# One score matrix per half in the expert retrieval: query weights times keys, built in the kernel, for heads 4 to 7 behind the first tile's sums

## What is computed

```python
def chunk(xc):                                    # xc: normed tokens
    q = (xc @ w_query).reshape(PEER_CHUNK, PEER_HEADS, 2, PEER_HALF)      # 8 heads, 2 halves, 128
    s = jnp.einsum('thcd,hckd->thck', q, keys)                            # 128 keys per half
    top_s, top_i = lax.top_k(s, PEER_TOPK)                                # 16 of each half
    cand_s = top_s[:, :, 0, :, None] + top_s[:, :, 1, None, :]
    cand_i = top_i[:, :, 0, :, None] * N_KEYS + top_i[:, :, 1, None, :]
    best_s, best_j = lax.top_k(cand_s, PEER_TOPK)                         # 16 of the 256 pairs
    idx = jnp.take_along_axis(cand_i, best_j, axis=-1)
    gate = jax.nn.softmax(best_s, axis=-1)
    act = gelu(jnp.einsum('thkd,td->thk', u_table[idx], xc))
    return jnp.einsum('thk,thkd->td', gate * act, v_table[idx])
```

## Time and profile before

| | us |
|---|---|
| median of 3 runs | 3325.18 (3314.89 to 3326.9) |
| the profiled execution, timed | 3328.39 |
| its span in the trace | 3326.6 |
| PE busy, in the span | 2289.7 |
| DVE busy | 2177.2 |
| ACT busy | 936.3 |
| POOL busy | 1330.7 |
| 1088 gathers, 1143 MB, share of 16 DMA engines | 84.0% of the span |

### The profile page before, as it was taken

How to read it: one execution, slowest core, us unless ns; L and a number is a source line. 1 busy time by engine, 2 the same in 40 slices (tenths; PEclk the granted TensorE clock), 3 DMA queues, 4 the chain that set the end, 5 groups by cost and what they waited for, 6 DMA issues and landing times.

```text
span 3326.6 us, 31891 instructions
## 1 busy us (share of the span) xinstructions
PE 2289.7 (69%) x9269; PEld 938.1 (28%) x9269; DVE 2177.2 (65%) x5175; ACT 936.3 (28%) x3200; POOL 1330.7 (40%) x1272
## 2 busy tenths in 40 slices
PE   8997675766685668566855685568566855685576
PEld 4555451331151115111511151115111511151121
DVE  4544539788667756775677567756776676568654
ACT  2222114323332222222322232322232223222222
POOL 1241014434443444344434443444444444444442
PEclk9999787886896779687978797889688978797799
DMA  5223269999999999999999999999999999999998
GB/s 192 84 72 88 75 270 358 386 386 402 419 419 415 417 400 417 416 417 402 419 416 417 400 419 415 416 398 419 413 413 418 419 402 420 397 408 411 420 420 338
DMA packets 188351, 1216.94 MB, mean 366 GB/s; under 512 B 27272, under 2 KB 30712, under 8 KB 47456
## 3 DMA queue, kind: packets, MB, share of 16 engines
q0 software_dynamic: 157600, 1143.05, 84.0%
q1 hardware_dynamic: 30576, 71.86, 6.0%
HBM read 1199.15 MB, written 15.55 MB: 365 GB/s over the span
## 4 chain that ended last, share of the span: by engine, by line
DMA 33%; PE 22%; DVE 17%; issue 7%; ACT 5%; POOL 3%; another core or an unknown queue 0%; DVEq 0%; POOLq 0%; PEldq 0%; ACTq 0%; SPq 0%
DMA uv_ring<-in_uv_table,idx 33%; PE ACC L1998 14%; DVE uv_ring L1823 9%; PE TQ L1937 5%; POOL uv_ring L1465 3%; ACT dg L1598 2%; PE OP L1918 1%; ACT dot L1591 1%; PE TQ L1959 1%; ACT dot L1578 1%; DVE pos L1668 1%; DVE idx_f L1744 1%; DVE pos L1665 1%; DVE S L1743 1%; DVE best L1667 0%
## 5 line engine op out<-in xcount | busy, mean ns | idle before, releaser
L1998 PE MATMUL ACC<-uv_ring,dg 128*64 128x512 f32 x4352 | 1440.2, 772 | 932.5 <-ACT dg L1598 932.3
L1465 POOL DMA_INDIRECT uv_ring<-in_uv_table,idx x1088 | 1234.1, 1134 | 1611.2 <-PE ACC L1998 1375.1
L1823 DVE CUSTOM_DVE_ANT_0 uv_ring<-uv_ring,xn 128x1024 f32<-128x1024 f32 x1088 | 1326.5, 1226 | 738.2 <-DMA uv_ring<-in_uv_table,idx 675.5
L1998 PEld LDWEIGHTS ACC<-uv_ring,dg 128*64 128x64 f32 x4352 | 339.4, 164 | 1925.4 <-ACT dg L1598 1405.6
L1578 ACT ACTIVATE dot<-dot 128x2 f32<-128x2 f32 x544 | 110.5, 203 | 1853.6 <-DVE dot L1823 1838.8
L1598 ACT ACTIVATE dg<-stack,dot 128x64 f32<-128x64 f32 x1088 | 326.4, 340 | 17.8
L1591 ACT ACTIVATE dot<-gate,dot 128x1 f32<-128x1 f32 x1088 | 261.1, 287 | 18.9
L1937 PEld LDWEIGHTS TQ<-glu_and_queries,wq 128*128 128x128 f32 x2048 | 237.0, 194 | 63.9 <-issue 63.9
L1937 PE MATMUL TQ<-glu_and_queries,wq 128*128 128x128 f32 x2048 | 250.5, 281 | 0.0
L527 PE MATMUL PJ<-w_in,xT 128*128 128x512 f32 (+1 forms) x384 | 142.7, 528 | 3.2 <-DVE pj L407 3.2
L527 PEld LDWEIGHTS PJ<-w_in,xT 128*128 128x128 f32 x384 | 72.2, 191 | 68.1 <-issue 65.2
(11 more groups left out here) (336 smaller groups left out, 1640.2 us busy)
## 6 DMA issues: line engine op xcount, KB each, us to landing
uv_ring<-in_uv_table,idx POOLq DMA_INDIRECT x1088
glu_and_queries<-in_w_glu SPq DMA_DIRECT2D x9, 1024.0 KB
wq<-in_w_query SPq DMA_DIRECT2D x8, 1024.0 KB, 19.5
w_in<-in_w_in SPq DMA_DIRECT2D x8, 640.0 KB, 11.0
xt<-in_x SPq DMA_DIRECT2D x9, 512.0 KB, 4.7
xr<-scratch_x SPq DMA_DIRECT2D x9, 512.0 KB
xc<-in_x_columns SPq DMA_DIRECT2D x8, 512.0 KB, 3.8
xk<-in_x SPq DMA_DIRECT2D x8, 512.0 KB, 3.5
```

The source lines that it names most:

```text
L1465: pool.indirect_dma_start(out=ring[:, s_ % RING, :], out_offset=None, in_=a["uv_table"], in_offset=bass.IndirectOffsetOnAxis(ap=idx[:, s_: ...
L1823: V.tensor_tensor_reduce(row, row, xn[:, g, :], 1.0, 0.0, ALU.mult, ALU.add, dot[:, s_:s_ + 1]).then_inc(dots, 1)
L1998: ins = nc.tensor.matmul(ACC[GT * g:GT * (g + 1), b, :], dg[:, n % DG, :], ring[:, n % RING, D + 512 * b:D + 512 * b + 512], start=False, ...
```

## The change

Scores are linear in the tokens: s = (x W) K^T = x (W K^T). The kernel after makes W K^T once, a matrix of 1024 x 128 for each of the 16 head halves (`score_w`), and each tile's scores come from `xnT` and `score_w` without queries. In detail:

- Host layout: the query weights are handed over turned, so that the part of 128 of a half's queries lies on partitions; the bytes are the same. `keys` comes in four blocks for two heads each, two of which fit in SBUF at a time.
- `make_weights(n)` builds a quarter of a head's weights: four matmuls of 128 columns, of a block of turned query weights and the keys, into one PSUM bank. `take_weights(n)` copies the bank over the query weights that it came from. For n under 16 (heads 0 to 3) the banks are the two of `ACC`; for later ones it is bank 1 of `TQ`.
- Heads 0 and 1 are built within tile 0's own preparation: head 0 behind the gating matmuls at (0, 9), head 1 behind the bottom projection at (2, 3). Heads 2 and 3 follow behind the scores of heads 0 and 1 and behind both `spread_rows`. Heads 4 to 7 are built behind tile 0's sums: at pairs 4 to 7, 10 to 13, 16 to 19, 22 to 25, one quarter a pair, and their scores in the two pairs behind each.
- Tile 0's scores of a head are eight matmuls of 256 columns. Later tiles: at the steps where queries stood, two matmuls of 512 columns a step, 32 in all; the copies to `S` stand at (3, 12) and (5, 0).
- VectorE: head 3's piece A moves from ahead of the first product to slot 7, pieces A of heads 4 to 7 from slots 10, 18, 27, 36 to 25, 37, 49, 61; B to D follow. C and C2 use 8 rows of `S` instead of twice 4 of `quarter`.
- Tile 1's steps follow a table, `FIRST_STEPS`: none up to slot 8, 50 up to slot 60, step 72 at slot 80, step 83 at slot 88, and 45 in the 30 slots behind.
- `w_glu` has memory of its own and is loaded once. On SP the first keys and head 0's query weights go ahead of `w_bot`, `xr` and `g_ffn`; head 1's follow. New waits: TensorE ahead of each quarter waits for an earlier copy (`taken`), and ahead of tile 1's transposes for all copies; ScalarE waits for `made`; ahead of the copy of tile 1's first scores it waits for all of tile 0's indices.

The core of the diff:

```diff
-        wq = c.sb("wq", [P, EH, KD, 2 * QH])
-        keys = c.sb("keys", [QH, HC, KEYS])
+        score_w = c.sb("score_w", [P, HC, KD, KEYS])
+        wq_rows = score_w[:].rearrange("p c k n -> p c (k n)")
+        keys = c.sb("keys", [QH, 2, 4, KEYS])
         w_bot = c.sb("w_bot", [P, SW // P, D])
-        glu_and_queries = c.sb("glu_and_queries", [P, 2 * KD * P])
-        w_glu = glu_and_queries[:].rearrange("p (k n) -> p k n", n=SW)
-        xnT = glu_and_queries[:, 0:KD * P].rearrange("p (k n) -> p k n", n=P)
-        qT = glu_and_queries[:, KD * P:].rearrange("p (k n) -> p k n", n=P)
+        w_glu = c.sb("w_glu", [P, SW // P, SW])
+        xnT = c.sb("xnT", [P, KD, P])
...
-            lo, hi = 3 * KS + 3, NSLOT - 10
-            return s_ if s_ < lo else min(NSLOT, lo + (s_ - lo) * (NSLOT - lo) // (hi - lo))
+            for (s0, n0), (s1, n1) in zip(FIRST_STEPS, FIRST_STEPS[1:]):
+                if s0 <= s_ < s1:
+                    return n0 + (s_ - s0) * (n1 - n0) // (s1 - s0)
+            return NSLOT
...
+        FIRST_STEPS = ((0, 0), (8, 0), (60, 50), (69, 59), (71, 64), (80, 72), (84, 80), (88, 83), (NSLOT - 10, NSLOT))
+        BEFORE = 4
+        LATE_AT = {e: 4 + 6 * (e - BEFORE) for e in range(BEFORE, EH)}
+        TOP_AT = {3: 7} | {e: 2 * at + 17 for e, at in LATE_AT.items()}
+        BEST_AT = {1: 3, 2: 9, 3: 16} | {e: at + 3 for e, at in TOP_AT.items() if e >= BEFORE}
+        FIRST_HEADS = {at + n: (e, piece) for e, at in BEST_AT.items()
+                       for n, piece in ((0, "B"), (2, "C"), (3, "C2"), (5, "D"))}
+        FIRST_HEADS |= {at: (e, "A") for e, at in TOP_AT.items()}
...
+                def load_keys(n):
+                    if n >= 2:
+                        sp.wait_ge(made, QUARTERS * 2 * (n - 1))
+                        sp.nop(nofuse=True)
+                    sp.dma_start(keys[:, n % 2].rearrange("d c n -> d (c n)"), a["keys"][n]).then_inc(keys_in[n % 2], 16)
+                def load_queries(e):
+                    sp.dma_start(wq_rows[:, 2 * e:2 * e + 2], a["w_query"][e]).then_inc(wq_in[e], 16)
...
+                load_keys(0)
+                load_queries(0)
                 sp.dma_start(w_bot[:], a["w_out"][AW:D, :].rearrange("(k p) n -> p k n", p=P)).then_inc(bottom, 16)
                 load_xr(0)
                 sp.dma_start(g_ffn[:], a["g_ffn"].to_broadcast([P, D])).then_inc(bottom, 16)
...
+                load_queries(1)
+                load_keys(1)
+                sp.dma_start(place[:].rearrange("p n k -> p (n k)"), a["place"].to_broadcast([P, 2 * KS])).then_inc(tables_in, 16)
+                sp.dma_start(spread[:].rearrange("p g n -> p (g n)"), a["spread"]).then_inc(tables_in, 16)
+                for e in range(2, EH):
+                    load_queries(e)
...
+                def take_weights(n):
+                    c_, k0 = n // 2, n % 2 * (KD // 2)
+                    src = ACC[:, n % 2, :] if n < QUARTERS * BEFORE else TQ[:, 1, :]
+                    act.wait_ge(made, n + 1)
+                    A(score_w[:, c_, k0:k0 + KD // 2, :].rearrange("p k n -> p (k n)"), src, ACT.Copy).then_inc(taken, 1)
+                def late_heads(pair):
+                    for e, at in LATE_AT.items():
+                        if at < pair <= at + QUARTERS:
+                            take_weights(QUARTERS * e + pair - at - 1)
+                        elif pair == at + QUARTERS + 2:
+                            first_scores(e)
+                            if e == EH - 1:
+                                for n in ("S_a", "S_b", "ex_done"):
+                                    act.sem_inc(k[n].sem, 1)
...
+                        if (h, j) == (0, 14):
+                            for n in range(QUARTERS):
+                                take_weights(n)
+                for n in range(QUARTERS, 2 * QUARTERS):
+                    take_weights(n)
                 prepare(0, 3, 2)
...
+                first_scores(0)
+                first_scores(1)
+                for g in range(GROUPS):
+                    take_rows(0, g)
+                for e in range(2, BEFORE):
+                    for n in range(QUARTERS * e, QUARTERS * (e + 1)):
+                        take_weights(n)
                     first_scores(e)
...
+                    if e == 2:
+                        first_gates(0)
...
-                        n = KS // 4
-                        for k0 in range(0, KS // 2, n) if piece == "C" else range(KS // 2, KS, n):
-                            dch_(V.tensor_tensor(quarter[:], first_cid[:].to_broadcast([P, n, NCAND]),
-                                                 bcast(pos_f[:, e, k0:k0 + n], NCAND, 2), ALU.subtract))
-                            dch_(V.tensor_reduce(idx_f[:, e, k0:k0 + n], quarter[:], AX.X, ALU.min, apply_absolute_value=True))
+                        n, k0 = KS // 2, KS // 2 * (piece == "C2")
+                        dch_(V.tensor_tensor(first_match, first_cid[:].to_broadcast([P, n, NCAND]),
+                                             bcast(pos_f[:, e, k0:k0 + n], NCAND, 2), ALU.subtract))
+                        dch_(V.tensor_reduce(idx_f[:, e, k0:k0 + n], first_match, AX.X, ALU.min, apply_absolute_value=True))
...
-                for e in range(1, 4):
+                for e in range(1, 3):
...
+                        n, bank, part = "ab"[h == 4], i // 4, i % 4
                         if i == 0:
                             k["xnT_done"].of(pe, t)
...
+                            if n == "a":
+                                k["zb_done"].of(pe, t)
+                                k["S_b"].of(pe, t - 1)
+                            else:
+                                k["S_a"].of(pe, t)
+                        c_ = 8 * (h == 4) + 4 * bank
+                        for m in range(2 * part, 2 * part + 2):
+                            ins = nc.tensor.matmul(ZS[:, bank, :], xnT[:, m, :], score_w[:, c_:c_ + 4, m, :],
+                                                   start=(m == 0), stop=(m == KD - 1))
+                        if i == 7:
+                            k[f"s_{n}"].mark(ins)
...
+                def make_weights(n):
+                    e, c_, k0 = n // QUARTERS, n // 2, n % 2 * (KD // 2)
+                    if n < QUARTERS * BEFORE:
+                        dst, free = ACC[:, n % 2, :], n - 1
+                    else:
+                        dst, free = TQ[:, 1, :], n
+                    if n % QUARTERS == 0:
+                        pe.wait_ge(wq_in[e], 16)
+                        pe.wait_ge(keys_in[e // 2 % 2], 16 * (e // 4 + 1))
+                    if free > 0:
+                        pe.wait_ge(taken, free)
+                    for m in range(KD // 2):
+                        ins = nc.tensor.matmul(dst[:, m * KEYS:(m + 1) * KEYS],
+                                               wq_rows[:, c_, (k0 + m) * P:(k0 + m + 1) * P],
+                                               keys[:, e // 2 % 2, c_ % 4, :], start=True, stop=True)
+                    ins.then_inc(made, 1)
+                def first_scores(e, m0, m1):
+                    b = e % 2 if e < BEFORE else 1
+                    if m0 == 0:
+                        pe.wait_ge(taken, QUARTERS * (e + 1))
+                        if e >= 2:
+                            pe.wait_ge(first["S"], e - 1 if e < BEFORE else e)
+                    for m in range(m0, m1):
+                        ins = nc.tensor.matmul(ZS[:, b, 0:2 * KEYS], xnT[:, m, :], score_w[:, 2 * e:2 * e + 2, m, :],
+                                               start=(m == 0), stop=(m == KD - 1))
+                    if m1 == KD:
+                        ins.then_inc(first["s"], 1)
+                def late_heads(pair):
+                    for e, at in LATE_AT.items():
+                        n = pair - at
+                        if 0 <= n < QUARTERS:
+                            if (e, n) == (BEFORE, 0):
+                                k["xn_taken_b"].of(pe, 0)
+                            make_weights(QUARTERS * e + n)
+                        elif QUARTERS <= n < QUARTERS + 2:
+                            m0 = (n - QUARTERS) * (KD // 2)
+                            first_scores(e, m0, m0 + KD // 2)
...
+                        if (h, j) in ((0, 9), (2, 3)):
+                            e = int(h == 2)
+                            for n in range(QUARTERS * e, QUARTERS * (e + 1)):
+                                make_weights(n)
                 k["xnT_done"].of(pe, 0)
...
+                pe.wait_ge(tables_in, 16 * 2)
+                first_scores(0, 0, KD)
+                first_scores(1, 0, KD)
+                for g in range(GROUPS):
+                    spread_rows(0, g)
+                for e in range(2, BEFORE):
+                    for n in range(QUARTERS * e, QUARTERS * (e + 1)):
+                        make_weights(n)
+                    first_scores(e, 0, KD)
```

148 lines of the change are left out of this document (43 added, 105 removed).

## The result

The changed kernel takes 3292.49 us (median of 5 runs, 3290.23 to 3297.64), the kernel before, in the same rounds, 3323.84 us (5 runs, 3314.89 to 3326.9). The ratio is 0.992, with a 95% interval of 0.9903 to 0.9938: faster by 31 us (21 to 32 by the interval), where 50 had been forecast. 3292.5 lies inside the range of 3257 to 3296, near its upper end. The profiled execution of the changed kernel has a span of 3290.7 us, against 3326.6.

What follows compares the result with a forecast made beforehand. The prediction took the stream of gathers on the DMA engines as the bound: its start, dry spells and other bytes. Gains of 27.5 (start), 6.5 (tile 0) and 16 us (later tiles) sum to 50, giving 3275 us, range 3257 to 3296.

Steps and rivals of the forecast that it cites:

- The start: From the beginning up to product 3: it starts at 471 instead of 498.5, 27.5 us earlier; bounds 16 to 30.
- (a): Start: head 0's weights, built behind the gating matmuls, are done by about 424.9; 2 us gained, of -3.1 to 2.9.
- (b): Start: loads queued ahead on SP make g_ffn land 3.1 us later, at 426.2; costs nothing, but only just.
- (c): Start, from xnT to head 0's scores: 8 matmuls gain 3 us at the full clock, about 0 at half.
- Slots 3 to 78: Tile 0, products 3 to 78: 197.5 us instead of 214.2, with VectorE's work below pace behind slot 15.
- all this lies beside other work: Tile 0: building matmuls, scores and copies added on TensorE and ScalarE fit beside a pair's pace of 5 us.
- limit of 5.4 us a pair: Tile 0: the prediction is wrong if pairs of slots with building matmuls pass 5.4 us.
- rival (1): Slots 79 to 117 cost more: tile 0 takes 345 us, 13 more, total 3288; chance 0.12.
- Rival (4): Tile 0: the hand-over of weights between TensorE and ScalarE goes serial, a loss of 15 us, 3340; chance 0.04.
- Rival (3): Start: no early start, through slow clock, late w_bot and ScalarE's standstill; 11 us lost, 3286; chance 0.08.
- Later tiles: After tile 0: six w_glu loads fewer in a full stream, 2.5 to 2.9 us each, save 16 us; bounds 0 and 20.
- Rival (2): Later tiles: the removed w_glu loads were hidden, so 16 us more, 3291; chance 0.08.

Runs made afterwards that it cites:

- e8: Kernel before, with both halves of the normed tokens spread early, behind head 1's queries, so products can start early: 3317.4 us, ratio 0.9991.
- e14: Changed kernel without query weights, their loads, building or copies, and with 16 ring places instead of 8: 3272.4 us, one run.
- e1: Changed kernel without the building of heads 4 to 7 behind tile 0's sums (matmuls and copies left out): 3293.4 us, ratio 0.9919.
- e10: Changed kernel without VectorE's match of numbers for heads 1 to 7 of tile 0: 3291.7 us, ratio 0.9910.
- e13: Changed kernel without query weights, their loads, building or copies, still with 8 ring places: 3301.5 us, one run.
- e15: Changed kernel, not edited, measured once more: 3295.6 us, ratio 0.9919.
- e2: Changed kernel with tile 1's preparation steps ahead of the late heads' building or scores in TensorE's order: 3292.0 us, ratio 0.9909.
- e3: Changed kernel with the choice of heads 3 to 7 in tile 0 split into two pieces on VectorE: 3292.7 us, ratio 0.9917.
- e4: Changed kernel with the load of w_glu put back, nine loads instead of one: 3313.5 us, ratio 0.9983.
- e16: Changed kernel with VectorE's two additions that wait for TensorE (and the gate's sigmoid on ScalarE) later in order, all tiles: 3286.7 us, ratio 0.9886.
- e7: Changed kernel with four edits: tile 1's steps first on TensorE, choice split, ScalarE's score copies a pair later, even steps from slot 70: 3291.9 us, ratio 0.9915.

## Why the prediction was right in parts and wrong in the sum

**The start: right, 27.0 us for a forecast of 27.5.** (a) Head 0's weights were in place at 424.4 (423.77 + 0.60; forecast 424.9), the clock stood at 1.00 in every stretch from 418 to 460, and the bottom matmuls took 7.13 us instead of 8.74. By the Trainium skill, "TensorE: Matmul & The Clock Gate", section "Part 1: The HAM clock gate (the "warmup" mystery)", activity lifts the clock from its throttled default; this trace agrees, 2.4 GHz in 424 to 426, where before it was 1.2. (b) g_ffn came at 426.06, as forecast (426.2), and here it was the last: TensorE idled 1.34 us for it. (c) From xnT to head 0's scores it took 440.37 to 444.50, 4.1 us instead of 7.1: 3.0, as forecast. Gather 0 came at 456.51, 1.5 us ahead of the forecast, mostly by something that no edit touches: the gating matmuls took 5.38 us instead of 6.72, as the clock stood at 1.00 from 418 on, where before had 0.50 up to 420. Gather 8 came at 474.05 (forecast 474), with DMA full from 470 to 510. Part of this was luck. Before's 498.5 held the standstill of 9.03 us, which the prediction knew and counted as gone, with a bound of 16 should it come again. It didn't come in this profile; it did, shorter, in four later ones. Of the 27.0 about 8.6 are this accident and some 18 the change, by the estimate under e8.

**Slots 3 to 78: the step that failed.** The prediction said: "in the 63 slots behind, it lies below pace, 157.5; and 5 us for waits as for the scores now (5.2): 197.5". It compared VectorE's total with the pace's total over 63 slots and took the larger. The change in VectorE's total was right; the rule isn't, with eight places. Before's own row spoke against it, 214.2 us for a pace of 190 and 174.7 busy, and taking 10 us of work away was no reason for that gap of 24 to fall to 7.5. A place goes round from its gather (9.4 us from issue to landing, the median in this stretch) through the wait for its product, ScalarE's diagonals, a pair's sums on TensorE and back to GpSimd. Eight slots at pace are 20 us, so all the rest together has 10, and its steps alone take about 5 of them (product 1.15, GELU, weights and diagonals 1.3, a pair's sums 1.9, the issue 0.9). The 9.4 is not a fixed time: it holds waiting behind other gathers, and was 6.2 where the ring had nearly run dry (gather 56) and 26.2 in e14. So the delay that costs nothing is an estimate, some 5 us with the one figure and 8 to 9 with the other. What exceeds it on any engine is lost, and a light stretch behind it doesn't give it back. That is why the lumps and waits of three engines count together, why taking away 14 us of TensorE's work (e1) or 16 of VectorE's (e10) was worth 2 to 3 us, and why sixteen places were worth 8.0. The missing 14.4 us are, by the runs taken in this order, 6.3 for the weights (e13: loads, building and copies out) and 8.0 for the bridging (e14): 14.3, which leads to 197.6 for a forecast of 197.5. That they meet so closely is partly luck, as the 197.5 held 5 us of waits.

Its other half, "all this lies beside other work", failed with it. A pair's matmuls fit beside the pace, 1.9 + 1.2 of 5 us, but not where late scores and tile 1's gating meet (5.6 us between two sums). The limit of 5.4 us a pair held for heads 4 to 6: 4.5, 5.3 and 4.9 for their four building pairs. Head 7's took 26.6 / 4 = 6.7, in the stretch with both bottom matmuls and the wait for xr; by its own words the prediction was wrong there.

The number of rival (1), 345 us for tile 0, is what came (345.8), and the place it named is not: it put the loss in the squeezed stretch.

**Slots 79 to 117: right**, 111.0 for 111. Where VectorE's work is dense and the bound, summing it up works. Rival (4), the serial hand-over, did not occur: ScalarE waited 6.4 us in all for building matmuls in slots 3 to 78, TensorE 2.2 us for its copies. Rival (3) didn't either, in this profile.

**Later tiles: right in the sum**, 16.1 us in the profiled pair, 13.0 with e15's profile instead, 20 to 23 with those of e1, e2, e3 and e10; the bounds were 0 and 20. e4 gives 1.7 to 3.4 us a load by the profile that it is compared with and 3.0 by the medians. That agrees with 2.5 to 2.9 and can't sharpen it. Rival (2), hidden loads, is out. By the Trainium skill, "DMA: Bandwidth & Descriptors", section "Anatomy of one DMA — SWDGE (gpsimd) path", the estimate had been 4.4 us a load; the page's fit is of DMAs that GpSimd issues, and these loads are SP's. Every price measured here lies below it, so the measurement decides. By these runs a load in a full stream costs about its bytes, and none shows 2 us on top.

**The total.** Forecast for the profiled pair 50, measured 35.9; the difference is the 14.4 of slots 3 to 78, with 0.5 more at the start and 0.8 back elsewhere. The medians differ by 31.4: the profiled execution of before, 3328.4 us as timed, was 4.6 above the median of its five runs, the one of after was at its median. Before's standstill, 8.6 us, may be the reason; no other execution of before was profiled. Without it the pair would differ by some 27 us.

**What stays open.** What ScalarE stood still for, and how often. Why the waits at a tile's end shrink with the additions moved (e16) and where its 9 us lie. And how the 8.0 us divide among the single lumps: the edits that smooth them don't add up (e7), and no kernel with all of the work came below 207.

## What to carry to other kernels

Where a stream runs through a few buffers, don't compare each engine's total work with the stream's pace over a long stretch. Add up, for one buffer, everything it passes through on all engines, and compare this with buffers x pace; what is left over is the longest delay that costs nothing, here 5 to 9 us. Take the landing time of a transfer that has few others ahead of it, since in a full queue it grows with the number of buffers. Work added to an engine that idles half the time is free only as long as this holds. Put an instruction that waits for another engine as late in its engine's order as its user allows: moving two additions by two and three slots was worth 9 us, while halving lumps or taking out 16 us of VectorE's work didn't move the median. And look for a standstill in each profile of a pair before reading their difference.

## What the runs showed that I had not expected

- The same stretch of one program repeats to 0.1 us in tile 0 (211.91 and 211.90), while the untouched first part of the kernel ends anywhere from 404.2 to 414.9 us over the profiles. Comparing lengths of stretches shows differences that medians of four runs hide, in tile 0. It also misleads: behind product 128 unedited tiles differ by up to 10 us, and a standstill of ScalarE in one profile and not in the other looked like a gain of the early rows.
- A DMA share of 0.97 doesn't mean 97% of the full rate: in slots 3 to 78 it came with 380 to 389 GB/s, and 1.01 with 419. Where the ring runs dry now and then, the share shows less than half of the loss; bytes over time show all of it.
- Twice the ring places shortened only tile 0 and the first tile behind it (335.2 and 318.8 us from product to product, control 347.7 and 327.6); from then on the tiles took 327 to 328 us, with eight places 327.7 to 330.3.
